# Gathered u and v rows as pairs, gates scatter-added in memory, and the dense expert stage split into an up pass and a down pass

## What is computed

```python
def _peer(h, wq, subkeys, u, v):
    q = (hf @ wq).reshape(n, PEER_HEADS, 2, PEER_QUERY_DIM // 2)
    s = jnp.einsum('nhpd,hpkd->nhpk', q, subkeys).astype(jnp.float32)
    sv, si = lax.top_k(s, PEER_TOPK)
    ...
    top_v, top_pos = lax.top_k(cand, PEER_TOPK)
    experts = jnp.take_along_axis(cand_idx, top_pos, axis=-1)
    gates = jax.nn.softmax(top_v, axis=-1).astype(h.dtype)
    ...
        act = jax.nn.gelu(jnp.einsum('td,tkd->tk', xb, u[eb]), approximate=False)
        return jnp.einsum('tk,tkd->td', gb * act, v[eb])
```

## Time and profile before

| | us |
|---|---|
| median of 3 runs | 3949.14 |
| lowest, highest run | 3946.01, 3950.29 |
| span of the profiled execution | 3944.0 |
| PE busy in it | 3668.8 (93%) |
| DVE busy | 2582.7 (65%) |
| POOL busy | 1645.1 (42%) |
| ACT busy | 732.8 (19%) |

### The profile page before, as it was taken

The page is one execution under the profiler, slowest core; times in us unless marked ns, Lnnn a source line. Parts: engine busy times, 40 slices in busy tenths (PEclk is TensorE's granted clock), DMA queues, the critical chain, the costliest instruction groups (busy, mean ns, idle before and its releaser), DMA issues. The chain is left out here.

```text
span 3944.0 us, 39966 instructions
## 1 busy us (share of the span) xinstructions
PE 3668.8 (93%) x13726; PEld 2099.9 (53%) x13726; DVE 2582.7 (65%) x5929; ACT 732.8 (19%) x1622; POOL 1645.1 (42%) x1498
## 2 busy tenths in 40 slices
PE   2988888999999999999989887889999999999997
PEld 1545676655555555555445566765555555555543
DVE  5685688777666666677724738878677646556344
ACT  1143355400000000000012535552000000000000
POOL 0030155446556644444502003544777655445340
PEclk7998999999999999999999998999999999999999
DMA  6321234579999999999930131447999999989774
GB/s 218 126 101 46 90 86 145 185 289 405 379 379 369 378 373 378 379 372 353 393 138 2 47 121 54 126 136 256 359 410 410 387 354 354 366 337 359 304 290 160
DMA packets 365386, 1026.96 MB, mean 260 GB/s; under 512 B 30849, under 2 KB 132481, under 8 KB 364417
## 3 DMA queue, kind: packets, MB, share of 16 engines
q0 software_dynamic: 147456, 536.94, 35.5%
q1 hardware_dynamic: 118000, 433.99, 28.9%
q10 hardware_dynamic: 99728, 53.48, 4.8%
HBM read 965.07 MB, written 59.22 MB: 260 GB/s over the span
## 5 line engine op out<-in xcount | busy, mean ns | idle before, releaser
L1859 PE MATMUL ps<-colsT,arena 128*128 128x384 f32 x4096 | 1359.0, 486 | 5.6 <-DMA arena<-in_peer_ut 5.6
L1859 PEld LDWEIGHTS ps<-colsT,arena 128*128 128x128 f32 x4096 | 775.8, 190 | 584.4 <-issue 94.7
L1894 PE MATMUL ps<-arena 128*128 128x512 f32 x1536 | 676.5, 592 | 0.0
L1366 POOL DMA_INDIRECT proj<-in_peer_u,eidx x336 | 478.9, 1425 | 240.9 <-DVE modbc L1560 110.5
L1366 POOL DMA_INDIRECT proj<-in_peer_v,eidx x335 | 361.1, 1078 | 312.7 <-DVE colsT L1571 214.5
L1894 PEld LDWEIGHTS ps<-arena 128*128 128x128 f32 x1536 | 291.8, 190 | 345.2 <-issue 317.6
L1352 POOL TENSOR_SCALAR x<-iota,modbc 128x128 f32<-128x128 f32 x192 | 145.2, 771 | 719.3 <-ACT modbc L1692 551.5
L1560 DVE CUSTOM_DVE_ANT_0 proj<-proj,rows 128x1024 f32<-128x1024 f32 x336 | 399.4, 1222 | 59.0 <-DMA proj<-in_peer_u,eidx 57.2
L1571 DVE SCALAR_TENSOR_TENSOR colsT<-proj,modbc,colsT 128x1024 f32<-128x1024 f32 x330 | 410.1, 1286 | 14.4 <-DMA proj<-in_peer_v,eidx 13.1
L1894 PE MATMUL ps<-arena,rows 128*128 128x512 f32 x768 | 337.8, 592 | 0.0
L1894 PE MATMUL ps<-arena,x 128*128 128x512 f32 x768 | 337.7, 592 | 0.0
(11 more groups left out here) (298 smaller groups left out, 3716.3 us busy)
## 6 DMA issues: line engine op xcount, KB each, us to landing
arena<-in_peer_ut SPq DMA_DIRECT2D x256, 512.0 KB
arena<-in_peer_v SPq DMA_DIRECT2D x256, 512.0 KB
gmat_d<-arena ACTq DMA_DIRECT2D x24, 2048.0 KB, 9.3
arena<-gmat_d SPq DMA_DIRECT2D x64, 768.0 KB
proj<-in_w_adaT SPq DMA_DIRECT2D x48, 512.0 KB
modbc<-in_w_adaT SPq DMA_DIRECT2D x30, 512.0 KB, 3.7
rows<-in_w_adaT SPq DMA_DIRECT2D x18, 512.0 KB, 3.5
arena<-in_w_in SPq DMA_DIRECT2D x2, 4224.0 KB, 16.6
```

What stands on the lines that cost most here:

```text
L1366: pool.indirect_dma_start(ring[slots[at]], None, tab, bass.IndirectOffsetOnAxis(ap=eidx[:, b * SLOTS + q:b * SLOTS + q + 1], axis=0)).then ...
L1859: mm = pe.matmul(ps[:, 2 + j % 2, 0:ND], utab[:, j % UR, k], hT[:, k, NG:T], start=(k == 0), stop=(k == KT - 1))
L1894: mm = pe.matmul(ps[:, Y_BANKS[2 * d + c2], :], wT[j % CR][:, d * P:(d + 1) * P], vtab[:, j % VR, c2 * 512:(c2 + 1) * 512], start=(j == 0) ...
```

## The change

- The dense part becomes two passes. In the **up pass** all 128 u stages run first; each gelu goes into a ring of 5 (`hidden`), and SP writes it to memory (`act_d`, 192 KB a j). In the **down pass** SP reads hidden tiles, gate tiles (192 KB a j each) and v tiles, DVE multiplies, and PE runs the 128 v stages.
- The placement is gone. A gate matrix in memory (`gate_d`, one per layer, 25.2 MB) is zeroed from ACT's queue in the mixer (6 DMAs from attention step 8 on, each 64 x 128 x 128 floats in pieces of 512 bytes). After a block is routed, POOL adds each of its 128 gates per token into it with an indirect DMA of 128 single floats (`scatter`), in groups of 16; each group waits until the one before has landed. 384 such DMAs a layer.
- u and v of an expert lie side by side in memory (`peer_uv`), and one gather brings both, 8 KB a token and 1 MB a DMA. The 256 gathers a layer (`fetch`) come on POOL after all scatters. The ring has 9 slots for the first 18 pairs and 5 after that.
- A pair is processed at once: DVE takes the dot (`dot`), ACT its gelu and the product with the gate (`weigh`), DVE adds the v row (`add_row`) two pairs later. 26 pairs stand in the up pass (ACT: `weigh(n)` behind the gelu of j = 100 + n), 230 in the down pass (`pairs_upto`: 230 over 120 j).
- The modulation tiles of the next layer (layer 0 only) are handled between the 26 pairs of the up pass; their loads stand in SP's queue from j = 105 on.
- x of the dense blocks stays in place, so its way out and back (`x_d`) goes.

```diff
-UR, VR, GR = 3, 3, 3
-A_GRP, B_TOK = 4, 16
+UR, AR, VR, WR, GR = 4, 5, 4, 10, 5
+ZERO_JS = 64
+ZERO_DMAS = JBLK // ZERO_JS * 3
...
                 for s in range(PSTEPS):
+                    if ZERO_STEP <= s < ZERO_STEP + ZERO_DMAS:
+                        j0 = (s - ZERO_STEP) // len(DB) * ZERO_JS
+                        d0 = (s - ZERO_STEP) % len(DB) * P
+                        act.dma_start(gate_d[l][j0:j0 + ZERO_JS][:, :, d0:d0 + P].rearrange("j i t -> i j t"),
+                                      zeros[:, :].unsqueeze(1).to_broadcast([P, ZERO_JS, P])).then_inc(g_zeroed, 16)
...
+                act.wait_ge(g_zeroed, 16 * ZERO_DMAS)
...
+        BASE = len(pairs_ring)
+        pairs_ring += [region(arena, 8192 + q * 2 * D, 2 * D) for q in range(4)]
+        RING = len(pairs_ring)
...
+        LAG = 2
+        PAIR_J, N_U, N_WIDE = 100, 26, 18
+        HEADS_FIRST, PAIRS_HEAD = 24, 0
+        ADA_PAIR = [4 + 4 * n // 9 for n in range(NMOD)]
+        ADA_J = [PAIR_J + ADA_PAIR[max(n - 2, 0)] + 1 for n in range(NMOD)]
...
+        def slot(n):
+            return n % RING if n < N_WIDE else n % BASE
...
+        def pairs_upto(j):
+            return min(NPAIRS, N_U + ((NPAIRS - N_U) * (j + 1) + 119) // 120)
...
                 for j in range(JBLK):
-                    load_u(U_AHEAD + UR + j)
+                    keep_hidden(j)
+                    load_u(UR + j)
...
+                    if j == JBLK - 4:
+                        sp.wait_ge(row_used, N_WIDE)
+                        sp.wait_ge(q_mm, NQ)
+                        for q in range(VR):
+                            load_v(q)
+                        for q in range(WR):
+                            load_hidden(q)
+                for j in range(GR):
+                    load_g(j)
+                for j in range(JBLK):
+                    load_g(GR + j)
                     load_v(VR + j)
+                    load_hidden(WR + j)
...
+                def scatter(d, h):
+                    b = DB[d]
+                    n = d * PH + h
+                    if h == 0:
+                        pool.wait_ge(ij_ready, d + 1)
+                    else:
+                        pool.wait_ge(g_sent, SENT0 + 16 * TOPK * n)
+                    for q in range(TOPK):
+                        s = b * SLOTS + h * TOPK + q
+                        pool.indirect_dma_start(gate_flat, bass.IndirectOffsetOnAxis(ap=eidx[:, s:s + 1], axis=0),
+                                                gates[:, s:s + 1], None, compute_op=ALU.add).then_inc(g_sent, 16)
...
+                def pair(n):
+                    if n < NPAIRS:
+                        dot(n)
+                    if n >= LAG:
+                        add_row(n - LAG)
+                        if (n - LAG) % SLOTS == SLOTS - 1:
+                            close_block((n - LAG) // SLOTS)
...
+                def weigh(n):
+                    i, q = n // SLOTS, n % SLOTS
+                    b = GB[i]
+                    one = dots[:, i, q:q + 1]
+                    act.wait_ge(dot_made, n + 1)
+                    c.link(act.activation(one, one, ACT.Gelu))
+                    act.activation(coef[:, i, q:q + 1], one, ACT.Copy,
+                                   scale=gates[:, b * SLOTS + q:b * SLOTS + q + 1]).then_inc(coef_made, 1)
...
+                    if PAIR_J <= j < PAIR_J + N_U:
+                        if j == PAIR_J:
+                            act.wait_ge(routed, 1)
+                        weigh(j - PAIR_J)
...
                 for j in range(JBLK):
-                    u_stage(U_AHEAD + j)
                     v_stage(j)
```

More of the change, by code:

```diff
@@ L1238, in build @@
-        slots = [slot(at) for at in range(NROWS)]
-        before = [max([p for p in range(at) if slots[p] == slots[at]], default=None) for at in range(NROWS)]
-        def landings(at):
-            return 16 * (landed_before[slots[at]] + slots[:at].count(slots[at]) + 1)
-        def rows_upto(j):
-            return min(NROWS, (9 * (j + 1) + 1) // 2 if j < JBLK - U_AHEAD else 450 + (9 * (j - JBLK + U_AHEAD + 1) + 3) // 4)
-        GELU_AT = [min(j for j in range(JBLK) if rows_upto(j) >= SLOTS * (b + 1)) for b in range(len(GB))]
@@ new lines, in build @@
+        PAIR_J, N_U, N_WIDE = 100, 26, 18
+        STEPS = 10
+        SC_PE = {7: 3, 13: 4}
+        SC_OUT = {6: 2, 12: 3, 21: 4}
+        EXP_AT = {11: 1, 19: 2, 29: 3, 40: 4}
+        HEADS_FIRST, PAIRS_HEAD = 24, 0
[3 more added lines that the diff above has]
+            return n % RING if n < N_WIDE else n % BASE
+        slots = [slot(n) for n in range(NPAIRS)]
+        before = [max([p for p in range(n) if slots[p] == slots[n]], default=None) for n in range(NPAIRS)]
@@ L1354, in _ @@
[L1354 to L1367 removed]
+                gate_flat = gate_d[l].rearrange("j i t -> (j i t)").rearrange("(n o) -> n o", o=1)
@@ L1369, in _ @@
+                n = 0
+                for i in range(len(DB) * PH):
+                    scatter(i // PH, i % PH)
+                    if i >= HEADS_FIRST:
+                        for _ in range(PAIRS_HEAD):
+                            fetch(n)
+                            n += 1
+                while n < NPAIRS:
+                    fetch(n)
+                    n += 1
             @block.vector
@@ L1528, in _ @@
                 normed(1)
-                for step in range(STEPS):
-                    route(0, step)
-                    if step == 1:
-                        residual(2)
-                    if step == 2:
-                        mean(2)
-                    if step == 3:
-                        normed(2)
-                    if step == 7:
-                        residual(3)
-                    if step == 8:
-                        mean(3)
+                route(0, 0)
+                residual(2)
@@ new lines, in _, with late_dots @@
+                route(1, 1)
+                mean(4)
+                route(1, 2)
+                normed(4)
+                route(1, 3)
+                gated(0)
+                for k in range(1, NB):
+                    for step in range(4 if k == 1 else 0, STEPS - 1):
+                        if k > 1 and step == 4:
+                            gated(k - 1)
+                        route(k, step)
+                dve.wait_ge(g2_landed, 16)
+                def late_dots(n):
+                    if n == 0:
+                        dve.wait_ge(silu_landed, 32)
+                    dve.wait_ge(w_landed[n % 2], 16 * (n // 2 + 1))
+                    ada_dots(dve, c, l + 1, n, late_ada[n % 2], late_silu, late_junk)
@@ L1613, in _ @@
+                for n in range(N_U):
+                    pair(n)
+                    if n == 3:
+                        gated(NB - 1)
+                    if l + 1 < depth:
+                        for m in range(NMOD):
+                            if ADA_PAIR[m] == n:
+                                late_dots(m)
                 if l + 1 < depth:
```

572 lines of the change are left out of this document (203 added, 369 removed).

## The result

The changed kernel takes **4860.32 us** (median of 4 runs, 4852.95 to 4862.31) against 3949.72 us (4 runs, 3946.01 to 3954.50): 1.230 times as long, 95% interval 1.228 to 1.232. Forecast were 4283 us and a range that ended at 4500. The direction was right and the size was not. The profiled execution took 4852.95 us and has a span of 4851.1 us, 907 more than before.

The account below looks back on a forecast made before the run. TensorE was taken to bound the kernel before, DMA the down pass after. Layer 0 (+207), layer 1 (+117) and zeroes (+10) took the 3944 us span to 4278; the median lies 5 above: 4283 us, range 4140 to 4500.

Parts of the forecast that it names:

- Scatters: On POOL, 24 groups of 16 a layer at 23 us a group, ending 691 us into the layer.
- the 25 us charged for POOL being held: Allowance in the scatters' sum for POOL being held beside routing, 25 us in all.
- Rival 1: Scatters on POOL dear: 40 us a group gives about 5030 us, 30 gives 4570; chance of more than 4500, 0.09.
- The "3" for landing: The 3 us added to each group of 16 scatters for waiting until the group before has landed.
- The ends of 21 and 40 us: Low and high limits given for the time of one scatter group on POOL, around the chosen 23 us.
- The order on ACT: Up pass: from j = 100 ACT's weigh waits for dot and gather; the next gelu, hidden store and u load wait behind.
- The tail behind the first pair: End of the up pass: 212 us of DVE work in layer 0 after the first pair lands at 697 us.
- Down pass: DMA becomes the bound at 3.85 us a pair, 917 us a layer against 654 us of PE work.
- a second limit lies close: Down pass: the ring of five slots gives 3.4 us a pair, or 4.2 us under load.
- rival 4: Faster than before: down pass not bound by DMA, at DVE's 2.81 us a pair, 682 us; 3812 us in all, chance 0.03.
- Zeroes: Zeroing the gate matrix from ACT's queue in the mixer: 5 us a layer charged, ends 0 and 89 us.
- the prediction's last sign: ACT waiting around attention step 9 would mean that the zeroes hold its queue.

Follow-up runs that it names:

- e2: The changed kernel with scatters that write instead of adding, same number of DMAs and same waits: 4418.60 us.
- e5: The changed kernel with no pair in the up pass, all 256 in the down pass, and the modulation columns done before the pairs: 4681.18 us.
- e6: The changed kernel with seven ring slots instead of five for the pairs of the down pass: 4846.84 us.
- e9: The changed kernel with gathers of half rows, 4 KB a token instead of 8 KB, their number unchanged: 4621.78 us.
- e10: The changed kernel with half-row gathers (4 KB a token) and seven ring slots in the down pass: 4336.34 us.
- e1: The changed kernel with layer 1's zeroes written from SP's queue in layer 0's up pass instead of ACT's queue in the mixer: 4836.06 us.
- e4: The changed kernel with layer 0's 48 modulation columns done before the first pair instead of between the 26 pairs: 4801.13 us.
- c3: The changed kernel with merged gates, plain scatters, 78 pairs spread over the up pass and zeroes moved: 4134.36 us, 1.048 times the kernel before.
- c1: The changed kernel, still with adding scatters, with 108 pairs fetched between scatters in the up pass and zeroes moved: 4375.13 us.
- c4: c3 with later places for exps and the last block's scores, and 100 up-pass pairs, eight a head: 4352.88 us, 1.100 times the kernel before.
- c5: c4 with other places for exps, the last block's scores and their copy: 4247.92 us, 1.078 times the kernel before.

## Why the prediction was wrong, point by point

**Scatters: the step that failed.** The prediction put "16 x 1.24 + 3 = 23 us a group", with 0.94 us and 0.30 us taken from gathers. The nearest row had the same engine and the same 128 pieces but not the same work: it does not add. A scatter that adds is issued in 1.55 us and a group takes 32.4 us ((1339 - 561)/24); a plain one takes 0.96 us, almost the gather's price. That is 9.4 us a group too little, 226 us a layer. The scatters also start at 137 us and not at 113, which the 25 us charged for POOL being held make good, and first pairs came 224 and 223 us late. With plain writes and nothing else changed (e2) the scatters end where the forecast had them, and 434 of the 573 us are gone. The reason I gave for the low value, that DVE's routing is mostly one-input work, spoke of contention and not of the addition. The "3" for landing was right: 32.4 - 16 x 1.85 = 2.8 us. The Trainium skill's page DMA: Bandwidth & Descriptors, section Anatomy of one DMA, gives about 2.0 us fixed; the trace agrees with it for that part (the waits for landing are 89.6/42 = 2.1 us). The page gives no price for the addition. Rival 1 is what came, between its 30 and 40 us a group, with its sign, gathers later than 750 us into a layer (915); I gave it 0.09. Its reason, "a scatter adds in memory", was the right one and got no price of its own. The ends of 21 and 40 us held the measured 32.4; the choice of 23 between them leaned on likeness, and no row made 30 us less likely. (The sums of the prediction hold to 1 us, but for rival 1: it leaves out the 25 us for POOL being held, and with them 30 us a group gives 4619 us and not 4570.)

**The order on ACT was right**, and with it that TensorE stops at j = 100 plus what it has in hand. e5 shows it: without these waits the u stages end 817 us into both layers. The forecast's own figure for that, 795, was 21 us short, all of it in the start of the u stages (122 us for 101); the stages themselves took 695 us against 694. After the change this miss lies under the wait for the scatters.

**The tail behind the first pair** was 255 us in layer 0 (212 forecast) and 147 in layer 1 (123). In both layers TensorE has 368 matmuls left, 23 u stages, 118 us at 5.14. Its first one comes late, at 1359.01 in layer 0 and 3783.62 in layer 1, 13.7 and 13.6 us behind the first dot, since a gelu, a store and a load lie between. The sum had no such restart, none of the short waits for u tiles behind it (five of 1.2 us in layer 1), and no lowered clock: the 368 matmuls are busy for 122.9 us in layer 1 and 146.5 in layer 0. In layer 0 DVE is busy for only 170 of 255 us; its gaps stay unexplained.

**Down pass: right.** 917 us forecast, 909 and 914 measured; 3.76 us a pair in its middle (213 gathers in 800 us) against the 3.85 chosen and the 3.72 from bytes alone, at 398 to 411 GB/s in the full slices of the page. The DMA engines bind, as the sum had it, and not the ring (e6); the ring is next (e9, e10), as "a second limit lies close" said. The fast rival 4 needed a gather not bound by DMA; with half the bytes the pass does take 665 us, so its mechanism was sound and its condition absent. About 410 GB/s is what the DMA reaches here at most (413 in one slice of e6, no more in any slice of any page). The Trainium skill's page DMA: Bandwidth & Descriptors, section Where 436 GB/s comes from, gives ~358 for HBM, a stack's rate divided by two cores. With the kernel on one core the traces go beyond it in every down pass with whole rows, so it was no bound here.

**Zeroes: mis-sized.** 10 us in the sum, 80 measured, inside the bound of 89 a layer that I had named for "if six queued DMAs hold ACT". They do hold it, and ACT waits behind attention step 8 as the prediction's last sign said (e1). I had costed the bytes against the time to the next out_proj, and not the queue of the engine that issues them.

## What to carry to other kernels

Before costing a DMA that a row does not show, ask what the issuing engine does for it that the nearest row's DMA does not; where nothing answers, give the upper price its full chance, above all with hundreds of them in a row on one engine. Look for the wait with the longest single time, follow it to the engine that was busy, and ask what else needs the same result: taking away single waits gained 22 us (e1), 52 (e4) and 172 (e5), while the scatters kept their hold. Several large transfers in small pieces, issued close together on a compute engine's queue, can cost that engine their issue: here 45.3 us of ACT.

## What the runs showed of the hardware

- An indirect DMA of 128 single floats holds POOL for 1.55 us when it adds and 0.96 us when it writes, with the same wait for landing behind a group (89.6 and 91.1 us in all); a gather of 128 rows holds it 0.93 us at the least and 1.0 in the median, at 8 KB a row (after) as at 4 KB (e9). The size of the row does not enter, the addition does.
- The same adding DMA takes 2.0 to 2.3 us where DVE multiplies and sums two operands beside it: 27.7 us more over 384 of them (e4).
- A 4 MB zeroing DMA in 512-byte pieces is issued in 0.37 us as the first, 4.26 as the second and 16.47 us as the third within 22 us, on ACT's queue. As 12 DMAs of 2 MB started five steps earlier the median issue is 0.37 us and the longest 7.04 (c3), and the first out_proj of layer 0 came at 393 and 391 us (c1, c3) instead of 424.
- TensorE's granted clock was 0.51, its lower level (1.2 of 2.4 GHz), in the holes, where it stood, and 0.80 and 0.93 over the windows behind them, in which it stood for their first 9 and 14 us.
- Matmuls issued one by one, mostly with 2.0 us between them, in two kernels (c4, c5), unexplained.
